# Memory and context rows loaded column-major, with their norms spread by a product, in a three-layer transformer kernel

## The reference

```python
def memory_cross_attention(q, mem, mem_g, w_mem_kv, q_g, k_g):
    mk, mv = jnp.split(rms_norm(mem, mem_g) @ w_mem_kv, 2, axis=-1)
    ...
def rms_norm(x, g):
    y = xf * lax.rsqrt(jnp.mean(xf * xf, axis=-1, keepdims=True) + EPS)
    return (y * g.astype(jnp.float32)).astype(x.dtype)
...
hc = modulate(rms_norm_2(ctx, g_pre_mix[layer]), csh_m, csc_m)      # h * (1 + scale) + shift
qa_c, ka_c, va_c, qr_c, kr_c, vr_c, gr_c = project(hc, w_in[layer], ...)
```

## Time and profile before

| | |
|---|---|
| median of 3 runs | 916.51 us (915.85 to 916.59) |
| profiled execution | span 915.7 us, 0.8 below the median |
| PE busy | 895.7 us, 98% |
| DVE busy | 696.4 us, 76% |
| ACT busy | 510.8 us, 56% |
| POOL busy | 82.6 us, 9% |
| moved by DMA | 175.61 MB, mean 192 GB/s |
| granted PE clock, mean | 0.999 |

### The profile page before, as it was taken

One profiled execution on the slowest core, in us unless ns is written; L12 is line 12 of the kernel. 1 busy time (PEld: TensorE's weight loads), 2 busy tenths in 40 slices (PEclk: granted clock), 3 DMA queues, 4 the chain that ended last, 5 costly groups with the idle time before them and its releaser, 6 DMA issues.

```text
span 915.7 us, 13893 instructions
## 1 busy us (share of the span) xinstructions
PE 895.7 (98%) x5112; PEld 753.3 (82%) x5112; DVE 696.4 (76%) x1094; ACT 510.8 (56%) x896; POOL 82.6 (9%) x81
## 2 busy tenths in 40 slices
PE   7999999999999999999999999999999999999997
PEld 5898978899788788988889887877787688888885
DVE  5789989879777468789798865878757779877553
ACT  5666574655445555555577546656645755555441
POOL 1301221100001011112121000100001100000000
PEclk9999999999999999999999999999999999999999
DMA  9654644745664755767866755463223568866641
GB/s 330 225 183 139 241 145 145 252 141 184 240 242 142 251 164 188 271 211 268 289 208 220 259 180 171 117 193 93 92 93 113 154 198 269 285 191 186 193 158 47
DMA packets 102788, 175.61 MB, mean 192 GB/s; under 512 B 7165, under 2 KB 32194, under 8 KB 102722
## 3 DMA queue, kind: packets, MB, share of 16 engines
q1 hardware_dynamic: 99856, 167.27, 55.7%
q0 software_dynamic: 2560, 7.31, 2.5%
q10 hardware_dynamic: 306, 0.14, 0.1%
HBM read 173.61 MB, written 1.06 MB: 191 GB/s over the span
## 4 chain that ended last, share of the span: by engine, by line
PE 84%; DVE 9%; ACT 3%; issue 2%; DMA 1%; POOL 1%; ACTq 0%; DVEq 0%; POOLq 0%
PE acc L1259 15%; PE acc L1261 15%; PE acc L1260 14%; PE acc L1321 9%; PE acc L1270 5%; PE acc L1272 5%; PE acc L1271 5%; PE acc L1322 4%; DVE wlo L2071 3%; PE tp L1416 1%; PE spsum L1400 1%; PE opsum L1536 1%; PE spsum L1403 1%; DVE macc L2321 1%; PE tp L1450 1%
## 5 line engine op out<-in xcount | busy, mean ns | idle before, releaser
L2071 DVE TENSOR_TENSOR wlo<-raw,whi 128x1024 fp32r<-128x1024 f32 (+2 forms) x274 | 325.2, 1194 | 105.4 <-ACT whi L1661 104.6
L1661 ACT CAST whi<-raw 128x1024 fp32r<-128x1024 f32 (+2 forms) x274 | 278.0, 1026 | 104.5 <-PE acc L1261 59.6
L1259 PE MATMUL acc<-whi,xx 128*128 128x512 f32 (+1 forms) x352 | 143.7, 408 | 1.9 <-DVE xx L2576 1.0
L1261 PE MATMUL acc<-whi,xx 128*128 128x512 f32 (+1 forms) x352 | 136.5, 388 | 0.0
L1260 PE MATMUL acc<-wlo,xx 128*128 128x512 f32 (+1 forms) x352 | 135.9, 386 | 0.0
L1321 PE MATMUL acc<-xx,whi 128*128 128x512 f32 x352 | 125.0, 399 | 0.8 <-DVE xx L2561 0.8
L1270 PE MATMUL acc<-xx,whi 128*128 128x256 f32 x384 | 113.0, 294 | 0.0
L1272 PE MATMUL acc<-xx,whi 128*128 128x256 f32 x384 | 108.6, 283 | 0.0
L1271 PE MATMUL acc<-xx,wlo 128*128 128x256 f32 x384 | 108.5, 283 | 0.0
L2646 POOL TENSOR_TENSOR small<-small,half_neg 128x8 f32<-128x8 f32 (+4 forms) x31 | 50.3, 1623 | 548.4 <-DVE small L2032 288.0
L1322 PE MATMUL acc<-xx,wlo 128*128 128x256 f32 x352 | 98.7, 280 | 0.0
(11 more groups left out here) (412 smaller groups left out, 1411.9 us busy)
## 6 DMA issues: line engine op xcount, KB each, us to landing
raw<-in_e_w_in SPq DMA_DIRECT2D x56, 512.0 KB, 5.6
raw<-in_o_w_in SPq DMA_DIRECT2D x56, 512.0 KB, 5.7
raw<-in_w_mod SPq DMA_DIRECT2D x48, 512.0 KB, 4.4
raw<-in_w_ffn_in SPq DMA_DIRECT2D x44, 512.0 KB, 5.0
raw<-in_w_in SPq DMA_DIRECT2D x28, 512.0 KB, 3.9
raw<-in_w_ffn_out SPq DMA_DIRECT2D x22, 512.0 KB, 4.3
raw<-in_e_w_out SPq DMA_DIRECT2D x16, 512.0 KB, 6.5
raw<-in_o_w_out SPq DMA_DIRECT2D x16, 512.0 KB, 4.6
```

The source lines that it names most:

```text
L1259: mm(o, hi, whi[:, slot, k, 0:pan.ncols], start=a, stop=False)
L1261: last = mm(o, lo, whi[:, slot, k, 0:pan.ncols], start=False, stop=z)
L1661: nc.scalar.copy(slab(whi, s.i % SPLIT_SLOTS, 0, s.nk, n), slab(raw, s.raw.i % RAW_SLOTS, s.koff, s.nk, n)).then_inc(S["hi_ready"], 1)
L2071: tt(slab(wlo, slot, 0, s.nk, n), slab(raw, s.raw.i % RAW_SLOTS, s.koff, s.nk, n), slab(whi, slot, 0, s.nk, n).bitcast(F32), ALU.subtract) ...
```

## The change

The host hands over two more arrays, `mem_t` and `ctx_t`: memory and context transposed, laid out as 128 partitions of eight blocks of 256 tokens, so that a column of the matrix lies in a partition. Each is 1 MB, loaded beside the rows and not in their place. The rows are still loaded (memory's now into `g2`), but only for the squares. The factor of each token is then needed along the free axis, the same in all partitions. `turn_diag` (DVE) writes the identity times the factors, `turn_spread` (PE) multiplies `ones` with it, and ACT copies the 128 x 256 result from PSUM to `spread`; `turn_scale` (DVE) multiplies the column-major data by it in place, four blocks at a time. `turned_part` replaces `rows_T` on ACT and DVE, and has nothing on PE. For memory the norm and scaling are made once and `turned_parts` used twice; `mem_t` goes to `h_res`, `ctx_t` to the place of `slo`.

```diff
+    def turned_rows(self, src, loaded, turned_loaded, pos, bank):
+        st = self.step("turn_stat", src=src, waits=loaded)
+        self.tick(st, "sq_ready", "ms_ready", "rstd_ready")
...
+        self.at(pos, lambda: self.tick(self.step("turn_diag", first=st, src=src), "diag_ready"), 1)
+        self.at(pos + 1, spread, 1)
+        for half in range(2):
+            self.at(pos + 2, lambda half=half: scale(half), 1)
...
     pl.step("load_mem")
     pl.at(0, lambda: pl.step("setup_gains"))
+    pl.at(2, lambda: pl.step("load_mem_t"))
     W = "e_w_in"
     evs = [pl.panel(W, 0, CW, "x", "norm", gs=64, dst=("g0", 0))]
-    stm = pl.norm_rows("h", "h", ("loaded_h", 16))
-    pl.transposed(stm, "side", ROW["e_mem"], pos=[pl.pos + 5 + q for q in range(4)], banks=("tp", "o") * 2)
+    pl.turned_rows("h", ("loaded_mem", 16), ("loaded_h", 16), pl.pos + 2, "tp")
+    pl.turned_parts("h", "side", ROW["e_mem"], None, [pl.pos + 5 + q for q in range(4)])
...
-    pl.transposed(stm, "side", ROW["o_mem"], pos=[b - 8, b - 7, b - 4, b - 3], banks=("s1", "s1", "s0", "s0"))(
-        lambda: pl.load("x", rows=pl.count["rt_ps"]))
+    pl.turned_parts("h", "side", ROW["o_mem"], None, [b - 8, b - 7, b - 4, b - 3])(
+        lambda: pl.load("x", rows_lo=pl.count["rt_lo"]))
...
     def context():
-        st = pl.norm_rows("g2", "g2", ("loaded_ctx", 16))
-        pl.transposed(st, "side", "ctx_A", "ctx_B", pos=[pl.pos + n for n in (3, 4, 6, 7)], banks=("s0", "o", "s0", "s1"))
+        pl.turned_rows("side", ("loaded_ctx", 16), ("loaded_ctx_t", 16), pl.pos + 2, "s0")
+        pl.turned_parts("side", "side", "ctx_A", "ctx_B", [pl.pos + n for n in (5, 6, 7, 8)])
...
+            def turn_spread(st):                                  # PE
+                pe.wait_ge(S["diag_ready"], st.on["spread_ps"])
+                wait(st.free[st.bank])
+                mm(bank_of(st.bank)[:, 0, :], ones, diag, start=True, stop=True).then_inc(S["spread_ps"], 1)
...
+            def turn_stat(st):                                    # ACT
+                before_squares(st)
+                wait(st.waits)
+                for t in range(NT):
+                    ins = f(scr[:, :], rows_of["g2"][:, t, :], ACT.Square, accum_out=stat(st, 0)[:, t:t + 1])
...
+            def turned_part(st):                                  # ACT
...
+                wait(("turned_ready", st.turned))
+                if st.bias is None:
+                    for k in range(2):
+                        last = f(hi[:, k, :], x[:, k0 + k, :], ACT.Copy, scale=a[:, k0 + k:k0 + k + 1])
...
+            def turn_diag(st):                                    # DVE
+                wait(("rstd_ready", st.first.on["rstd_ready"]))
+                for t in range(NT):
+                    last = ts(diag[:, t * P:(t + 1) * P], ident, stat(st.first, 2)[:, t:t + 1], None, ALU.mult)
+                last.then_inc(S["diag_ready"], 1)
+
+            def turn_scale(st):                                   # DVE
+                wait(st.waits)
+                wait(("spread_sb", (st.on["turned_ready"] + 1) // 2))
+                x = turned[st.src][:, 4 * st.half:4 * st.half + 4, :]
+                tt(x, x, spread.unsqueeze(1).to_broadcast([P, 4, T]), ALU.mult).then_inc(S["turned_ready"], 1)
...
             def load_mem(st):                                     # POOL
                 pool.wait_ge(S["raw_loaded1"], 16)
-                pool.dma_start(h_res[:, :, :], w["mem"].rearrange("b (t p) d -> p (b t) d", p=P))\
-                    .then_inc(S["loaded_h"], 16)
+                pool.dma_start(rows_of["g2"], w["mem"].rearrange("b (t p) d -> p (b t) d", p=P))\
+                    .then_inc(S["loaded_mem"], 16)
+
+            def load_mem_t(st):
+                wait(("sub_done", 1))
+                pool.dma_start(turned["h"].rearrange("p k t -> p (k t)"), w["mem_t"]).then_inc(S["loaded_h"], 16)
...
                 elif st.what == "ctx":
                     pool.dma_start(rows_of["g2"], w["ctx_2"].rearrange("b (t p) d -> p (b t) d", p=P)).then_inc(s, 16)
+                    wait(("sub_done", st.side))
+                    pool.dma_start(turned["side"].rearrange("p k t -> p (k t)"), w["ctx_t"]).then_inc(S["loaded_ctx_t"], 16)
```

More of the change, by code:

```diff
@@ L334, in transposed, with spread, scale, turned_parts @@
         return after
+    def turned_rows(self, src, loaded, turned_loaded, pos, bank):
+        st = self.step("turn_stat", src=src, waits=loaded)
+        self.tick(st, "sq_ready", "ms_ready", "rstd_ready")
+        self.uses(st, "scr", "sq_ready")
+        def spread():
+            self.tick(self.step("turn_spread", first=st), "spread_ps", "spread_sb")
+            self.uses(self.steps[-1], bank, "spread_sb")
+            self.steps[-1].bank = bank
+        def scale(half):
+            x = self.step("turn_scale", half=half, src=src, waits=turned_loaded)
+            self.tick(x, "turned_ready")
+        self.at(pos, lambda: self.tick(self.step("turn_diag", first=st, src=src), "diag_ready"), 1)
+        self.at(pos + 1, spread, 1)
+        for half in range(2):
+            self.at(pos + 2, lambda half=half: scale(half), 1)
+    def turned_parts(self, src, key, scale, bias, pos):
+        def quarter(q):
+            st = self.step("turned_part", src=src, key=key, scale=scale, bias=bias, q=q)
+            st.turned = self.count["turned_ready"] - (q < 2)
+            self.tick(st, "rt_hi", "rt_lo")
+            if bias is not None:
+                self.uses(st, "scr", "rt_lo")
+                st.ready_cols = self.count["mcol_done"]
+            self.src[key] = st.on["rt_lo"], 4
+            if then and q == 3:
+                then()
+        then = None
+        for q in range(4):
+            self.at(pos[q], lambda q=q: quarter(q), 1)
+        def after(make):
+            nonlocal then
+            then = make
+        return after
     def transposed_by_k(self, xn, ready, key, scale, bias, pull=()):
@@ L588, in residual, with load @@
         return [(n, self.count[n]) for n in ("resid_done", "post_done") if n in self.count]
-    def load(self, what, after=0, rows=0):
+    def load(self, what, after=0, rows=0, rows_lo=0, turned=0):
         st = self.step("load", what=what, after=after, rows=rows)
+        st.rows_lo, st.turned = rows_lo, turned
         self.tick(st, "loaded_" + what)
@@ L722, in make_plan @@
     evs.append(pl.panel("o_w_mem_kv", CW, CW, "side", "copy", dst=("g1", 2)))
+    side_read = len(pl.subs)
     pl.tile_ready = {}
@@ L754, in make_plan @@
             assert not pl.pending["g2"]
-            pl.load("ctx", after=pl.count["o_ps"])
+            pl.load("ctx", after=pl.count["o_ps"]).side = side_read
             pl.load("rope", after=pl.count["o_ps"])
@@ L771, in make_plan @@
     assert not pl.pending["g0"]
-    pl.load("post_mix", after=pl.count["o_ps"], rows=pl.count["rt_ps"])
+    pl.load("post_mix", after=pl.count["o_ps"], turned=pl.count["turned_ready"])
     assert m <= pl.pos + 4, (m, pl.pos)
@@ L1144, in program @@
                    "gates": gflat[:, 0:2048].rearrange("p (t d) -> p t d", t=NT)}
+        turned = {"h": h_res[:, :, :].rearrange("p t d -> p (t d)").rearrange("p (k t) -> p k t", t=T), "side": ctx_t[:, :, :]}
+        diag, spread = g2[:, 0:T], g2[:, T:2 * T]
         gq = sidef[:, 0:1024].rearrange("p (j t) -> p j t", t=T)
@@ L2703, in _ @@
             pool.wait_ge(S["setup_pool"], 1)
-            does = {"load_mem": load_mem, "mod_row": mod_row, "forget_sum": forget_sum, "forget_rows": forget_rows, "load": load}
+            does = {"load_mem": load_mem, "load_mem_t": load_mem_t, "mod_row": mod_row, "forget_sum": forget_sum, "forget_rows": forget_rows, "load": load}
             for st in pl.steps:
@@ L2745 @@
     w_out = named["w_out_2"]
+    for name, a in (("mem_t", named["mem"]), ("ctx_t", named["ctx_2"])):
+        named[name] = np.ascontiguousarray(a[0].T.reshape(KT, P, T).transpose(1, 0, 2).reshape(P, KT * T))
     named["w_out_2"] = np.concatenate([w_out[:, 0:512].reshape(1, 2, 4, 64, D).swapaxes(1, 2).reshape(1, 512, D),
```

53 lines of the change are left out of this document (47 added, 6 removed).

## The result

The changed kernel takes 919.23 us (median of 8 runs, 918.51 to 920.62) where the kernel before takes 916.55 (8 runs, 915.85 to 917.08): ratio 1.0029, 95% interval 1.0020 to 1.0039, so 1.8 to 3.6 us slower. Forecast was 917.0 with a range up to 919.0. The time is outside that range, and slower had been given 0.20.

What follows compares the result with a forecast made beforehand. PE was taken as the bound (busy 98%, 84% of the chain). Terms -5.28 + 0.87 + 2.7 + 2.15 = +0.44 us on 916.51 gave 917.0 us, range 912.9 to 919.0.

Steps and rivals of the forecast that it cites:

- slower: Rival, chance 0.20: in the context `ctx_t` holds the engines, DVE falls 4 us behind instead of 1.6; 919.4 us.
- What is removed, what is added on PE: PE's own sum: twelve transpose blocks off, -5.28 us; two products of `ones` x `diag` added, 0.87; together -4.4.
- the transposes' rival: Rival, chance 0.05: transposes cost their records' 272 ns each, so 13.1 us come off instead of 5.3; 909.2 us.
- First norm, the wait for `diag`: At the memory's norm, PE reaches the product at 34.0, DVE finishes `diag` at 34.5: PE waits 0.5 us.
- First norm, the new 1 MB: `mem_t`, from about 19.5 to 24, delays weight slabs; first-norm stalls 2.7 us in all, against 1.33 saved.
- d: Delay of sub 6's weight slab by the memory's new transfer: between 0 and 2.7 us, taken as 2.2.
- The cover of 0.7 us: In the first norm, sub 7's split is done 0.7 us before PE wants it, absorbing that much of the slab's delay.
- In the middle group ... four blocks vanish, -1.76 us, and nothing is queued in their place.: Second use of the memory, 191 to 213: no new norm or product, four transpose blocks saved, -1.76 us.
- Context, `diag`: Second norm: 0.55 us wait for `diag` plus 1.6 lateness from `ctx_t` delaying weights; stalls 2.15 us against 1.33 saved.
- The `hi` and `lo` evacuations stay ... None of this has a price by itself.: Side engines: the evacuations now read SBUF; changed DVE and ACT work was given no price of its own.
- The sum: PE's removed and added work plus the stalls of both norms: +0.44 us on the kernel before.
- The 0.8 us "taken as constant": Run median 916.51 against the profiled span 915.7: 0.8 us outside the span, assumed unchanged.

Runs made afterwards that it cites:

- run 3: Changed kernel with only 64 of 2048 columns of each turned array loaded, the rest filled with ones by POOL: 915.13 us, ratio 0.9993.
- run 9: Changed kernel with both new transfers moved elsewhere and `load_mem_t` added to the planner's PASSABLE list: 915.48 us, ratio 0.9986.
- run 11: Memory as in run 9, context as in the kernel before: 915.41 us, ratio 0.9985.
- before again: The kernel before, unchanged, profiled again: span 913.9 us, ratio 1.0003.
- Run 12: run 9 with the second and third convolution tap cut to 64 columns, leaving DVE less work: one profiled run, 915.45 us.
- Run 5: Kernel before with the load of x waiting for the low parts on DVE, so issued later, at 213.50: ratio 1.0000.
- run 7: Changed kernel with only the memory's change kept and the context as in the kernel before: 917.15 us, ratio 1.0011.
- run 1: Kernel before with the two turned arrays handed over as inputs but never loaded: 916.31 us, ratio 1.0004.
- run 10: run 9 with the context's diag, spread, scaling and four parts each one sub earlier: 915.52 us, ratio 0.9990.
- run 2: Changed kernel with the turned data placed behind the rows in the same tensors, so no extra inputs: 918.43 us, ratio 1.0028.
- run 8: Changed kernel with both new transfers moved, the memory's later and the context's earlier: 915.85 us, ratio 0.9995.
- after again: The changed kernel, unchanged, profiled again on the same chip as before again: 920.51 us, span 917.3, ratio 1.0050.

## Why the prediction missed

*What is removed, what is added on PE.* Right for what is removed: four blocks of transposes less are 1.74 us in every variant, forecast 1.76, and the transposes' rival (their record's 272 ns) fell. The two products are there, but at 0.70 us each and not 0.43, with PE waiting before them.

*First norm, the wait for `diag`.* Forecast 0.5 without the transfer and 1.2 with it. It measured 0.7 in both traces with the transfer, 0.7 with small transfers (run 3) and in run 9, and 0.2 in run 11.

*First norm, the new 1 MB.* Mechanism right, and the size within the spread: d was taken as 2.2 and measured 1.5 and 2.8 by the earlier trace rows. Stalls 2.2 and 2.8 us against 2.7, net +0.81 and +1.53 against +1.37. How they divide was wrong: 1.5 and 2.1 on `wlo` and 0.7 on `diag`, against 1.5 and 1.2. The cover of 0.7 us was read in a trace in which PE stood 0.6 us later than in "before again", which has no such cover. That the net agrees is partly luck, as the stage itself moves by 0.7 us between traces.

*"In the middle group ... four blocks vanish, -1.76 us, and nothing is queued in their place."* This step failed. The saving was real and 0.82 to 0.85 of it was lost 25 us later. I looked at what is queued in the blocks' place on PE, and not at what else would soon be late: the timelines of ACT and DVE were read at the norms only, not between 208 and 235. Run 12 shows that DVE is the limit there: without 1.6 us of its work the stage gives back nothing (-0.02). Run 5 shows that the later load of x costs nothing in the kernel before.

*Context, `diag`.* Right: ACT's wait at 454, forecast to end near 455.1, ended at 454.36; stalls forecast 2.15, measured 1.7 and 2.3.

*"The `hi` and `lo` evacuations stay ... None of this has a price by itself."* This step failed too. From 486 to 504 the context loses 1.1 us more (0.5 and 0.2 as waits of PE on ACT; the rest is lost around these waits and is no row of its own). It is there with small transfers, with moved ones, and not with the old context (runs 7, 11), so it belongs to the context's steps, and not to the transfer. The four parts follow at four subs in a row and no longer at 3, 4, 6, 7, and each of their ACT pairs takes 1.09 us from `ctx_t`, where run 1's from PSUM take 1.02 to 1.06. Which of the two it is was not separated and stays open; moving the parts one sub earlier did not change the sum (run 10).

*The sum.* +0.44 forecast. The two missed terms, +0.83 and +1.1, give +2.4, and the measured +2.7 has that within its interval. The rival *slower* named the right side and the wrong mechanism: `ctx_t` made DVE's split 0.95 us later than in the earlier trace rows (455.44 for 454.49) and not 4. The range ended at 919.0, under the 919.4 of that rival, because I let every unknown lie in the stalls that I had found.

*Time outside the span.* The 0.8 us "taken as constant" was wrong: 1.8 everywhere. It did not enter the sum, but it made me test the inputs first (runs 1 and 2), and it hid that the trace of before was of a long execution.

## What to carry to other kernels

Where the busiest engine is relieved, the saving ends at the next engine that is full: look for it behind the edit, up to the next place where the two meet, and not only at the edit. A transfer that is small against the whole costs what the DMA engines lack where it is put: the same 2 MB cost 2.7 us of the trace where the change put them and about nothing in two other places (run 8 against run 3). Where a planner has a list of what may be passed, a new kind of step is an edit of the order too, even if it issues one instruction.

## What was not expected of the hardware

PE's rate in the last layer's products. From 735 to 805 a trace takes either the time of "before again" or 1.28 us more, with the same instructions, no waits, and the granted clock at 1.00 in both. The groups of the first product over 740 to 800, of the kernel after and of "after again":

```profile
L1368 PE MATMUL acc<-xx,whi 128*128 128x512 f32 x171 | 60.5, 399 | 0.0
```

```profile
L1368 PE MATMUL acc<-xx,whi 128*128 128x512 f32 x174 | 60.4, 394 | 0.0
```

In 60 us PE makes 171 of them or 174. The longer form is in the traces of before, after, and runs 5, 7, 11 and 12, the shorter in eleven others, and run 3's has 0.5 us more in one step near 800. The form goes with the execution and not with the kernel: before and before again differ, and so do after and after again. The cause stays open. Whoever compares two single traces of this kernel has 1.3 us of this in the difference or not, about half of what the change itself costs.
